# Gating units summed in PSUM from the first, the output norm moved ahead of them, and the next layer's shift read inside the last turn of branch a

## The chip, the cores and the metric

One core of one Trainium2 chip runs the whole program. The metric is the device time of that core in microseconds (us). The engines are TensorE (PE), VectorE (DVE), ScalarE (ACT), GpSimd (POOL) and SyncE (SP), which here only issues DMAs.

## What is computed

Two layers of a trunk with three branches, on 256 tokens of width 2048. Cut to what matters for the change:

```python
cond = jax.nn.silu(c)
for layer in range(DEPTH):                       # 2
    shift, scale, gate = split(cond @ w_ada[layer] + b_ada[layer])   # each 2048 wide
    h = rms_norm(x, norm_g[layer]) * (1.0 + scale) + shift
    ... = split_columns(h @ w_in[layer])         # a: delta rule, b: convolution, c: attention
    y_a = rms_norm(o_a, gdn_norm_g[layer]) * silu(z_a)
    y_b = silu(layer_norm(u, ...)) * silu(z_b)
    y_c = o_c * silu(z_c)
    merged = g_a * (y_a @ w_proj_a) + g_b * (y_b @ w_proj_b) + g_c * (y_c @ w_proj_c)
    x = x + gate * (merged @ w_out[layer])
```

The change touches three things: `cond @ w_ada` for `gate` (called GATING in the kernel) of each layer, where its first four row blocks are summed; the place of the output norm of `y_a`; and the place where the next layer's `shift` is read.

## The kernel before

**The weight stream.** All big products go over weights of 512 KB a slot (256 rows by 512 columns), in a ring of four buffers: SP loads `raw` (L365, once `w_split` says that the slot's last user on POOL is done), ACT rounds it to `wh` (L524, once PE has used the slot four back), POOL subtracts to get `wl` (L503, counts `w_split`), and PE multiplies three times (L864 to L866, counts `w_used`). A group over the model width is eight slots, a projection is four. All engines walk the 672 slots in the same written order. SP's queue is in order: whatever it waits for, all later loads wait behind it.

**The z groups and the branches.** In each layer, behind branch c, come two groups for z_b, two for z_a (`z_silu(4)` and `z_silu(5)` on DVE are for these), then four turns of branch b and four of branch a. A turn is a gate group of eight slots and a projection of four. DVE adds the gate bias when the gate group is done (`gate_add`, L1624), ACT takes its tanh (`gate_tanh`), which frees the PSUM banks of pair 0, and DVE merges (`merge`, L1637 and L1639). ACT rounds four slots ahead of PE, so `gate_tanh` of a turn stands behind its rounding of that turn's four projection slots.

**The conditioning units.** `cond @ w_ada` is summed on DVE, one block of 128 rows at a time: `mod_unit` (L1352 to L1362) waits for a 1 MB block in `modw0` or `modw1`, multiplies it by a column of `cond` and adds it to a running sum of 128x2048. The sum lies in PSUM (`ps[:, 4:8]`, called wide) or in SBUF (`acc`, called side). Units 0 to 3 go from SBUF to SBUF, on a sum set to zero first; unit 4 (`UNIT_A`) reads SBUF and writes PSUM; 5 to 14 stay in PSUM; 15 goes back to SBUF. Each counts `mod_used`. SP issues the load of block n (`mod_load`, L373 to L378) once unit n-2 has counted, because there are two buffers, and these loads stand in the same queue as the weight stream:

- blocks 0 and 1 of GATING in the last z_a group; blocks 2 and 3 behind slot 1 of the first gate group of b, blocks 4 and 5 behind its slot 5, 6 and 7 behind slot 1 of the projection, and so on;
- in the last turn of a of layer 0, the units of the next layer's SCALE: blocks 0 and 1 behind slots 1 and 5 of the gate group, 2 and 3 behind slot 1 of the projection.

Between them lies DVE's written order. Ahead of the b turns it is: `o_recip(0)` (half of the reciprocal for the output norm, L1801), a memset, `z_silu(4)`, the last steps of y_b (L1808, L1810), units 0 and 1, `o_recip(1)`, the output norm's multiply (L1816), `yl` (L1819), `z_silu(5)`, the multiply of y_a (L1822), units 2 and 3. In the last a turn of layer 0 it is: a wait for `mod_summed` and the read of the shift (L1366), a memset, units 0 and 1, `gate_add`, three `merged_low` (L1869), units 2 and 3, `merge`.

`mod_summed` comes from PE, which adds the 128 partitions of `acc` up with 16 small products (`mod_sum`, L958) ahead of the last slot (`MOD_T = 14`) of the gate group of that last turn. In the projection of that turn PE also turns the merged rows (`turn_merged`, L1269): the first before its second half slot, once `gate_tanh` has freed pair 0; the second needs `shift_taken` too, since the shift lies in the bank that it writes.

Of the kernel before, what the change touches and what calls it, by code (L numbers as in the profile page):

```python
# [20 lines left out]
ALU = mybir.AluOpType  # L21
# [107 lines left out]
def trunk(nc, xt, cvec, rel_bias, w_ada, w_in, w_pa, w_pb, w_pc, w_out, b_gate, params, consts, hot, out):  # L129
    ctx = ExitStack()  # L130
    with ctx:
# [1170 lines left out]
        def _(dve):  # L1302
# [49 lines left out]

            def mod_unit(kt, u, s, which, last=KT - 1):

                V.drain()
                dve.wait_ge(mod_landed[s], (u - s) * 8 + 16)
                side = acc[:, which].rearrange("p (b n) -> p b n", b=4)
                wide = ps[:, 4:8, :]
                V.scalar_tensor_tensor(wide if UNIT_A <= kt < last else side,  # L1359
                                       modw[s][:].rearrange("p (b n) -> p b n", b=4), cond[:, kt:kt + 1],  # L1360
                                       wide if UNIT_A < kt <= last else side, ALU.mult, ALU.add
                                       ).then_inc(sem("mod_used"), 1)  # L1362

# [30 lines left out]
            for layer in range(DEPTH):  # L1394
# [405 lines left out]
                def o_recip(half):  # L1800
                    V.reciprocal(ors[:, 4 * half:4 * half + 4], ors[:, 4 * half:4 * half + 4])  # L1801

                dve.wait_ge(sem("o_rms"), L1)
                o_recip(0)
                V.memset(acc[:, 0], 0.0)
                z_silu(4, 0, zs[0])
# [3 lines left out]
                V.scalar_tensor_tensor(ub[:], ub[:], 0.25, zs[1][:], ALU.mult, ALU.mult).then_inc(sem("yb_ready"), 1)  # L1810
                for n in (0, 1):
                    mod_unit(n, passes[0] + n, n % 2, 0)

                o_recip(1)
                V.drain()
                V.scalar_tensor_tensor(qg, qg, p_(layer, "gdn_g"), ors[:], ALU.mult, ALU.mult)  # L1816
                done("o_normed")
                dve.wait_ge(sem("yh_ready"), 3 * layer + 2)
                V.tensor_tensor(yl[:], ub[:], yh[:].bitcast(F32), ALU.subtract).then_inc(sem("y_split"), 1)  # L1819
                z_silu(5, 1, zs[0])  # L1820
                hc += 4 * G_IN
                V.scalar_tensor_tensor(qg, qg, 0.5, zs[0][:], ALU.mult, ALU.mult).then_inc(sem("ya_ready"), 1)  # L1822
                for n in (2, 3):
                    mod_unit(n, passes[0] + n, n % 2, 0)

                def turn(i, br, n0, last_a=False):

                    plan = turn_units(layer, br, i == 3)
                    if plan:
                        l, part, kt = plan  # L1830
                        at = passes[(part + 1) % 3] + kt
                        k0 = 0 if i == 3 else i * 4
                        if i == 3:
                            V.memset(acc[:, 1 - part], 0.0)
                    def units(first):
                        for n in range(first, first + 2):
                            if plan:
                                mod_unit(k0 + (kt + n), k0 + (at + n), n % 2, 0 if part == GATING else 1 - part)

                    units(0)  # L1840
                    gate_add(i, hc, n0)
                    if last_a:
                        return units
                    units(2)
# [14 lines left out]
                for i in range(3):  # L1859
                    turn(i, "a", 12 * layer + 8)  # L1860
                    merge(i, hc, 12 * layer + 8, False)
                if not last_layer:
                    dve.wait_ge(sem("mod_summed"), 3 * layer + 2)
                    mods_from(layer + 1, SHIFT).then_inc(sem("shift_taken"), 1)
                units = turn(3, "a", 12 * layer + 8, True)
# [71 lines left out]
```

## Time and profile before

| | |
|---|---|
| median of three runs | 2473.62 us (2473.61 to 2476.98) |
| the profiled execution | 2470.99 us, of which the span is 2469.2 us |
| granted TensorE clock, mean | 0.959 of full speed |
| instructions | 37923 |
| bytes moved | 479.83 MB, mean 194 GB/s |

The page of the profile gives busy time by engine; the timeline gives the instructions of one engine in order, merged where alike, with the idle time ahead in brackets and what ended it; the chain of waits groups idle time by who was waited for. SPq is SP's own queue: its rows are DMA issues. A row of the stretches view gives busy us of each engine with the number of instructions, then the granted clock, the share of the DMA engines' time and the rate.

### The profile page before, as it was taken

What the parts mean: (1) busy time and instruction counts of PE and PEld (TensorE: products, weight loads), DVE (VectorE), ACT (ScalarE), POOL (GpSimd) and SP (SyncE); (2) the same over time, 40 slices, a digit from 0 to 9 for tenths busy, and PEclk for the clock granted to TensorE, in tenths of its full rate; (3) what the DMA queues carried; (4) which work ended last, traced back from release to release, by engine and by line L of the source; (5) the groups of instructions that cost most, each with busy time, mean ns of one, the idle gap of its engine ahead of it and who ended that gap; (6) DMA issues with size and microseconds to landing.
All of it is one profiled execution on the core that took longest, in us unless ns stands there. A gap on an engine that the chain in (4) does not pass through costs nothing.

```text
span 2469.2 us, 37923 instructions
## 1 busy us (share of the span) xinstructions
PE 2293.0 (93%) x15224; PEld 2098.9 (85%) x15224; DVE 1250.3 (51%) x1742; ACT 949.4 (38%) x1014; POOL 1674.1 (68%) x676
## 2 busy tenths in 40 slices
PE   3789899989999979998896999998999999899999
PEld 3679899978889968786896999998788998688899
DVE  6749874745443474543434694764545437421110
ACT  2234344472332534343333444436423234344442
POOL 1358768755554778986775886876555558798876
PEclk7789999999999999999998999999999999999999
DMA  8877535443333569797774574554334335975664
GB/s 329 319 252 224 162 121 178 146 132 121 124 119 103 179 244 323 279 319 263 289 249 148 186 218 143 167 168 130 124 123 128 111 114 194 323 272 187 200 209 154
DMA packets 228326, 479.83 MB, mean 194 GB/s; under 512 B 21569, under 2 KB 25793, under 8 KB 219617
## 3 DMA queue, kind: packets, MB, share of 16 engines
q1 hardware_dynamic: 226880, 475.72, 57.2%
q8 instruction: 96, 1.57, 0.3%
q10 hardware_dynamic: 1312, 2.23, 0.2%
q14 instruction: 38, 0.30, 0.0%
HBM read 471.48 MB, written 6.29 MB: 193 GB/s over the span
## 4 chain that ended last, share of the span: by engine, by line
POOL 47%; issue 40%; PE 12%; POOLq 1%; DMA 0%; ACT 0%; DVE 0%; DVEq 0%; ACTq 0%
POOL wl L503 47%; PE ps L864 4%; PE ps L865 4%; PE ps L866 4%; POOLq L502 0%; PE ps L958 0%; DMA raw<-w_pb 0%; PE ps L1269 0%; POOLq L498 0%; ACT wh L524 0%; ACT gate L512 0%; DVE xs L1889 0%; DVE ps L1624 0%; POOLq L503 0%; DVEq L1307 0%
## 5 line engine op out<-in xcount | busy, mean ns | idle before, releaser
L503 POOL TENSOR_TENSOR wl<-raw,wh 128x1024 fp32r<-128x1024 f32 x672 | 1673.9, 2504 | 782.1 <-ACT wh L524 780.7
L524 ACT CAST wh<-raw 128x1024 fp32r<-128x1024 f32 x672 | 701.0, 1048 | 1275.2 <-PE ps L866 994.9
L864 PE MATMUL ps<-ah,wh 128*128 128x256 f32 x3008 | 873.3, 290 | 49.9 <-DVE al L1404 36.2
L865 PE MATMUL ps<-al,wh 128*128 128x256 f32 x3008 | 859.9, 286 | 0.0
L866 PE MATMUL ps<-ah,wl 128*128 128x256 f32 x3008 | 859.5, 286 | 0.0
L864 PEld LDWEIGHTS ps<-ah,wh 128*128 128x128 f32 x3008 | 587.0, 195 | 57.5 <-issue 22.5
L865 PEld LDWEIGHTS ps<-al,wh 128*128 128x128 f32 x3008 | 586.8, 195 | 4.7 <-issue 4.4
L866 PEld LDWEIGHTS ps<-ah,wl 128*128 128x128 f32 x3008 | 586.3, 195 | 0.0
L864 PE MATMUL ps<-wh,ah 128*128 128x512 f32 (+1 forms) x832 | 327.0, 393 | 28.1 <-POOL wl L503 28.1
L866 PE MATMUL ps<-wh,al 128*128 128x512 f32 (+1 forms) x832 | 320.0, 385 | 0.0
L865 PE MATMUL ps<-wl,ah 128*128 128x512 f32 (+1 forms) x832 | 319.9, 385 | 0.0
L864 PEld LDWEIGHTS ps<-wh,ah 128*128 128x128 f32 x832 | 158.3, 190 | 60.7 <-POOL wl L503 32.8
L1453 DVE SCALAR_TENSOR_TENSOR ps<-upad,par,ps 128x256 f32<-128x256 f32 x480 | 199.6, 484 | 9.0
L866 PEld LDWEIGHTS ps<-wh,al 128*128 128x128 f32 x832 | 158.0, 190 | 31.6
L865 PEld LDWEIGHTS ps<-wl,ah 128*128 128x128 f32 x832 | 158.3, 190 | 28.1
L864 PE MATMUL ps<-wh,yh 128*128 128x512 f32 x384 | 157.6, 411 | 2.1 <-POOL wl L503 2.1
L865 PE MATMUL ps<-wl,yh 128*128 128x512 f32 x384 | 151.6, 395 | 0.0
L866 PE MATMUL ps<-wh,yl 128*128 128x512 f32 x384 | 151.3, 394 | 0.0
L1624 DVE TENSOR_TENSOR ps<-ps,gbias 128x1024 f32<-128x1024 f32 x24 | 29.5, 1230 | 195.4 <-PE ps L866 195.4
L1359 DVE SCALAR_TENSOR_TENSOR ps<-modw,cond,ps 128x2048 f32<-128x2048 f32 x37 | 87.1, 2355 | 34.4 <-DMA modw<-w_ada 29.9
L1347 DVE SCALAR_TENSOR_TENSOR ps<-adaw,cond,ps 128x512 f32<-128x512 f32 x112 | 84.6, 755 | 9.2 <-issue 0.5
L864 PEld LDWEIGHTS ps<-wh,yh 128*128 128x128 f32 x384 | 73.5, 191 | 17.9 <-POOL wl L503 4.4
(254 smaller groups left out, 2057.7 us busy)
## 6 DMA issues: line engine op xcount, KB each, us to landing
raw<-w_in SPq DMA_DIRECT2D x512, 512.0 KB, 3.4
modw<-w_ada SPq DMA_DIRECT2D x64, 1024.0 KB, 5.7
adaw<-w_ada SPq DMA_DIRECT2D x32, 1024.0 KB, 7.5
raw<-w_out SPq DMA_DIRECT2D x64, 512.0 KB, 4.7
raw<-w_pc SPq DMA_DIRECT2D x32, 512.0 KB, 3.6
raw<-w_pb SPq DMA_DIRECT2D x32, 512.0 KB, 8.1
raw<-w_pa SPq DMA_DIRECT2D x32, 512.0 KB, 4.9
gbias<-b_gate SPq DMA_DIRECT2D x24, 256.0 KB, 4.2
```

What stands on the lines that cost most here:

```text
L503: nc.gpsimd.tensor_tensor(wl[:, s], raw[:, s], wh[:, s].bitcast(F32), ALU.subtract).then_inc(sem("w_split"), 1)
L524: A.copy(wh[:, s], raw[:, s]).then_inc(sem("w_rounded"), 1)
L864: M.matmul(o, lh, rh, start=start, stop=False, skip_group_check=True)
L865: M.matmul(o, lh, rr, start=False, stop=False, skip_group_check=True)
L866: return M.matmul(o, ll, rh, start=False, stop=last, skip_group_check=True)
L1347: u = V.scalar_tensor_tensor(o, adaw[j][:, m], cond[:, kt:kt + 1], wide, ALU.mult, ALU.add)
L1359: V.scalar_tensor_tensor(wide if UNIT_A <= kt < last else side, modw[s][:].rearrange("p (b n) -> p b n", b=4), cond[:, kt:kt + 1], wide if ...
L1453: V.scalar_tensor_tensor(o, upad[:, ct, back:back + T], w, o, ALU.mult, ALU.add)
L1624: V.tensor_tensor(ps[:, 0:2, :], ps[:, 0:2, :], spread(gbias[:], 1, [P, TT, GW]), ALU.add).then_inc(sem("gate_sum"), 1)
```

## The change

`mod_unit` gets an argument `first`, the unit from which the sum lies in PSUM: 0 for GATING, still `UNIT_A` for SHIFT and SCALE. Unit 0 of every pass becomes a plain multiply, and the memsets that set the sums to zero go, ahead of the b turns and in the last turn of b and a. The output norm goes ahead of `z_silu(4)`, units 0 and 1 stay where they were, unit 2 goes ahead of `z_silu(5)`, unit 3 stays. The read of the next layer's shift goes behind the first two units of the last a turn.

```diff
-            def mod_unit(kt, u, s, which, last=KT - 1):
+            def mod_unit(kt, u, s, which, last=KT - 1, first=UNIT_A):
                 V.drain()
                 dve.wait_ge(mod_landed[s], (u - s) * 8 + 16)
                 side = acc[:, which].rearrange("p (b n) -> p b n", b=4)
                 wide = ps[:, 4:8, :]
-                V.scalar_tensor_tensor(wide if UNIT_A <= kt < last else side,
-                                       modw[s][:].rearrange("p (b n) -> p b n", b=4), cond[:, kt:kt + 1],
-                                       wide if UNIT_A < kt <= last else side, ALU.mult, ALU.add
-                                       ).then_inc(sem("mod_used"), 1)
+                o = wide if first <= kt < last else side
+                w = modw[s][:].rearrange("p (b n) -> p b n", b=4)
+                if kt == 0:
+                    unit = V.tensor_scalar(o, w, cond[:, 0:1], None, ALU.mult)
+                else:
+                    unit = V.scalar_tensor_tensor(o, w, cond[:, kt:kt + 1], wide if first < kt <= last else side,
+                                                  ALU.mult, ALU.add)
+                unit.then_inc(sem("mod_used"), 1)
...
+                def gating_units(*n):
+                    for m in n:
+                        mod_unit(m, passes[0] + m, m % 2, 0, first=0)
+
                 dve.wait_ge(sem("o_rms"), L1)
                 o_recip(0)
-                V.memset(acc[:, 0], 0.0)
+                o_recip(1)
+                V.drain()
+                V.scalar_tensor_tensor(qg, qg, p_(layer, "gdn_g"), ors[:], ALU.mult, ALU.mult)
                 z_silu(4, 0, zs[0])
...
-                for n in (0, 1):
-                    mod_unit(n, passes[0] + n, n % 2, 0)
-
-                o_recip(1)
-                V.drain()
-                V.scalar_tensor_tensor(qg, qg, p_(layer, "gdn_g"), ors[:], ALU.mult, ALU.mult)
-                done("o_normed")
+                gating_units(0, 1)
                 dve.wait_ge(sem("yh_ready"), 3 * layer + 2)
                 V.tensor_tensor(yl[:], ub[:], yh[:].bitcast(F32), ALU.subtract).then_inc(sem("y_split"), 1)
+                gating_units(2)
                 z_silu(5, 1, zs[0])
                 hc += 4 * G_IN
                 V.scalar_tensor_tensor(qg, qg, 0.5, zs[0][:], ALU.mult, ALU.mult).then_inc(sem("ya_ready"), 1)
-                for n in (2, 3):
-                    mod_unit(n, passes[0] + n, n % 2, 0)
+                gating_units(3)
...
-                        if i == 3:
-                            V.memset(acc[:, 1 - part], 0.0)
...
-                                mod_unit(k0 + (kt + n), k0 + (at + n), n % 2, 0 if part == GATING else 1 - part)
+                                mod_unit(k0 + (kt + n), k0 + (at + n), n % 2, 0 if part == GATING else 1 - part,
+                                         first=0 if part == GATING else UNIT_A)
 
                     units(0)
+                    if last_a and layer < DEPTH - 1:
+                        dve.wait_ge(sem("mod_summed"), 3 * layer + 2)
+                        mods_from(layer + 1, SHIFT).then_inc(sem("shift_taken"), 1)
                     gate_add(i, hc, n0)
...
-                if not last_layer:
-                    dve.wait_ge(sem("mod_summed"), 3 * layer + 2)
-                    mods_from(layer + 1, SHIFT).then_inc(sem("shift_taken"), 1)
                 units = turn(3, "a", 12 * layer + 8, True)
```

## Rows read from the trace of the kernel before

**Rows 1.** The page's first part: busy us, share of the span, instructions.
```profile
PE 2293.0 (93%) x15224; PEld 2098.9 (85%) x15224; DVE 1250.3 (51%) x1742; ACT 949.4 (38%) x1014; POOL 1674.1 (68%) x676
```

**Rows 2.** SP's own waits, whole span: us, times, longest.
```profile
SPq L377 <- DVE acc L1359: 85.3, 15, 16.7
```

**Rows 3.** PE's waits, the stretch 825 to 945 us, then 2030 to 2150 us.
```profile
PE ps L864 <- POOL wl L503: 14.6, 6, 8.9
...
PE ps L864 <- POOL wl L503: 14.6, 6, 8.8
```

**Rows 4.** SPq's timeline ahead of layer 0's first b turn: start, us, issues.
```profile
867.59 4.75 SPq L377 DMA_DIRECT2D modw<-w_ada  x2
872.39 7.01 SPq L365 DMA_DIRECT2D raw<-w_in  x4
894.33 4.71 SPq L377 DMA_DIRECT2D modw<-w_ada  x2
899.09 0.95 SPq L365 DMA_DIRECT2D raw<-w_in  x2
```

**Rows 5.** DVE's timeline in the same stretch.
```profile
834.85 6.55 DVE L1801 RECIPROCAL ors<-ors 128x1024 f32<-128x1024 f32 x1 [3.63 <-ACT ors L797]
...
855.05 1.22 DVE L1608 SCALAR_TENSOR_TENSOR zs<-zt,ps 128x1024 f32<-128x1024 f32 x1 [11.51 <-ACT zt L512]
...
863.25 8.72 DVE L1359 SCALAR_TENSOR_TENSOR acc<-modw,cond,acc 128x2048 f32<-128x2048 f32 x2
...
881.27 4.28 DVE L1819 TENSOR_TENSOR yl<-ub,yh 128x2048 fp32r<-128x2048 f32 x1
...
886.83 3.10 DVE L1822 SCALAR_TENSOR_TENSOR qkv<-qkv,zs 128x2048 f32<-128x2048 f32 x1
890.04 8.63 DVE L1359 SCALAR_TENSOR_TENSOR acc<-modw,cond,acc 128x2048 f32<-128x2048 f32 x2
```

**Rows 6.** The unit's forms on DVE: ns least/median/most, first and last start.
```profile
L1359 DVE SCALAR_TENSOR_TENSOR ps<-modw,cond,ps x37: 2354/2355/2358, 903.5 to 2188.6; 128x2048 f32<-128x2048 f32 x37
L1359 DVE SCALAR_TENSOR_TENSOR acc<-modw,cond,acc x19: 2350/4259/4320, 863.3 to 2099.5; 128x2048 f32<-128x2048 f32 x19
```

**Rows 7.** POOL's subtraction: all of them, then four in the stretch of rows 5.
```profile
L503 POOL TENSOR_TENSOR wl<-raw,wh x672: 2332/2403/4477, 38.5 to 2454.0; 128x1024 fp32r<-128x1024 f32 x168
...
879.39 17.14 POOL L503 TENSOR_TENSOR wl<-raw,wh 128x1024 fp32r<-128x1024 f32 x4 [0.38 <-ACT wh L524]
```

**Rows 8.** ACT's timeline in the same stretch.
```profile
880.56 1.01 ACT L512 ACTIVATE zt<-ps 128x1024 f32<-128x1024 f32 x1
...
904.95 1.04 ACT L524 CAST wh<-raw 128x1024 fp32r<-128x1024 f32 x1 [20.21 <-DMA raw<-w_in]
```

**Rows 9.** Stretches of 5 us: busy (x) of PE, PEld, DVE, ACT, POOL; clock, DMA.
```profile
890.00:895.00 5.00, 3.64 (x16) 2.55 (x14) 4.85 (x2) 0.00 (x0) 5.00 (x2) 1.00 0.02 3
...
905.00:910.00 5.00, 1.54 (x4) 1.25 (x5) 0.84 (x1) 2.12 (x3) 3.93 (x2) 0.50 1.00 302
```

**Rows 10.** PE's wait in layer 0's last a turn, 1130 to 1210 us.
```profile
PE ps L1269 <- ACTq L735: 12.3, 1, 12.3
```

**Rows 11.** SPq's timeline there.
```profile
1142.27 2.73 SPq L365 DMA_DIRECT2D raw<-w_pa  x2
1161.74 2.78 SPq L377 DMA_DIRECT2D modw<-w_ada  x2
```

**Rows 12.** DVE's timeline there.
```profile
1135.85 1.22 DVE L1639 TENSOR_TENSOR mtok<-mtok,ps 128x1024 f32<-128x1024 f32 x1
1156.97 0.17 DVE L1366 TENSOR_TENSOR mods<-ps,par 128x16 f32<-128x16 f32 x1 [19.90 <-PE ps L958]
...
1159.36 4.79 DVE L1359 SCALAR_TENSOR_TENSOR acc<-modw,cond,acc 128x2048 f32<-128x2048 f32 x2
1164.08 1.23 DVE L1624 TENSOR_TENSOR ps<-ps,gbias 128x1024 f32<-128x1024 f32 x1
```

**Rows 13.** A stretch behind the wait of rows 10, columns as in rows 9.
```profile
1174.00:1178.00 4.00, 2.95 (x11) 2.76 (x12) 0.00 (x0) 0.95 (x2) 3.42 (x2) 0.50 0.96 399
```

## The prediction

> **What bounds the kernel now.** I read the page first. PE is busy 93% of the span and POOL, which has to subtract every weight slot before PE may use it, 68% [rows 1]. So no engine is full, and what the change can win is PE's idle time. Then I read SP's own waits: its load of the conditioning blocks stood 85.3 us behind units that DVE sums in SBUF, 16.7 us at the longest [rows 2]. While it stands there, no weight is loaded. Then PE's waits in three stretches: around the first b turn of layer 0 and of layer 1 PE's products waited 14.6 us for POOL, each time, 8.9 us of it at once [rows 3], and in the last a turn of layer 0 PE's turning waited 12.3 us for ACT's queue [rows 10]. The timelines say what lay behind both.
>
> *Ahead of the b turns.* SP may load blocks 2 and 3 only when units 0 and 1 have counted. These run from 863.25 to 871.97 on DVE [rows 5], so SP issues them at 867.6 and 872.0, and the next weights at 872.39 [rows 4]. Then come blocks 4 and 5, which need units 2 and 3: these run from 890.04 to 898.67, behind `o_recip(1)`, the norm, `yl`, `z_silu(5)` and the y_a multiply [rows 5]. SP issues weights until 879.40, and the next at 899.09 [rows 4]: 19.7 us without a weight load. ACT sits 20.21 us for it, until 904.95 [rows 8]. Between 890 and 895 us the DMA engines are at 0.02 of their time [rows 9]. So this is a wait and no shortage of bandwidth.
>
> *In the last a turn.* DVE is free at 1137.1, but its next instruction is the shift, for which it waits 19.90 us until PE has summed it, at 1156.97 [rows 12]. Units 0 and 1 stand behind, at 1159.36, and SP's load of block 2 behind unit 0. SP's weights stop at 1145.0 and go on behind 1164.5 [rows 11]. So projection slots 2 and 3 come late, ACT's tanh stands behind rounding them, and PE's first turn behind the tanh.
>
> **The change part by part.**
>
> *Units 0 and 1 of GATING in PSUM.* A unit from SBUF to SBUF takes 4.259 us in the median, one from PSUM to PSUM 2.355, always [rows 6]. The least of the SBUF form, 2.350, shows that the instruction itself is no longer; the rest is DVE and POOL in each other's way, for POOL's subtraction takes 2.403 in the median and 4.28 (17.14 / 4) in this stretch [rows 7]. The new unit 0 is a form that no row has, a plain multiply from SBUF to PSUM. Between zero and 4.32 (the most of rows 6) I take 2.36, for it moves the same 2048 elements with one input fewer. Units 0 and 1 then end at 863.25 + 2 x 2.36 + 0.1 = 868.1 instead of 872.0: SP goes on 3.9 us earlier, and the weights behind it too.
>
> The Trainium skill (SBUF — State Buffer, Who interferes with whom) says that a VectorE instruction with two SBUF inputs and a GpSimd one that reads SBUF lock each other out for the whole instruction. By that a contended pair would cost 2.36 + 2.40 = 4.76 us, where the rows show 4.26 and 4.28. The sum with it would be some 1 us better a layer for the units and 1.6 us worse for the y_a multiply, so it changes little; the measurement is used.
>
> *Output norm ahead of `z_silu(4)`.* Added there are 6.55 us for `o_recip(1)` [rows 5] and the multiply; L1822, of the same size, took 3.10. Together 9.65, under the 11.51 us for which DVE sat idle ahead of `z_silu(4)` [rows 5], with a memset less besides. So nothing in front. If that cover were gone, y_b and all behind it would be late by the excess, at most the 9.65. Behind units 0 and 1 it takes these 9.2 to 9.65 us out of DVE's order.
>
> *Unit 2 ahead of `z_silu(5)`.* DVE: `yl` from 868.2 to 872.5 (4.28, it is contended), then unit 2 to 874.9 if block 2 has landed. It is issued at 865.9 instead of 867.6. So unit 2 has counted before SP comes to block 4, which stands behind weight slots whose buffers come free only at about 877.5 (879.4 less some 2). Price: nothing, as `z_silu(5)` waits for its tanh meanwhile.
>
> *What is late next.* `z_silu(5)` needs ACT's tanh, which began at 880.56 [rows 8] behind the rounding of weights that SP had issued late. These come 3.9 us earlier at best. I take the tanh 3 us earlier, so over at 878.6, with the bounds 877.7 and 881.6 (not earlier at all). Then `z_silu(5)` 1.22, the y_a multiply 3.10, unit 3 2.36 and 0.3 between them: unit 3 counts at 885.6 (884.7 to 888.6) instead of 898.67. SP, which stood before block 5, and all the weights behind it go on **13.1 us earlier**, bounds 10.1 and 14.0. PE must also have used up what it had by then: it lost 1.9 us a slot to the four contended subtractions [rows 7], of which only one, under the y_a multiply, is left, so PE is some 5 to 7 us ahead there and still has to wait a little. From here each load, unit and slot follows the other as before, in DMA queues that fill as before [rows 9]. I take 12.5 a layer, a little under the 13.1, for a multiply that is contended in full. Layer 1 has the same instructions and waits [rows 3], so 2 x 12.5 = **25.0 us**, bounds 20 and 28.
>
> After 9 us of idle PE's clock was at 0.50 of full speed, the lower of its two levels, between 905 and 910 us [rows 9]. With an idle time of some 3 us it may stay up, and one weight slot less run at half speed. That would be about 1.8 us a layer. I leave it out of the sum, since the projection slots behind then wait for loads in a full queue, and keep it for the range: 3.6.
>
> *The shift inside the turn.* Units 0 and 1 of SCALE now start at 1137.1, as their blocks stand in SP's queue ahead of the weights of 1142.27 [rows 11] and units 14 and 15 of SHIFT have long been done. They are still summed in SBUF, at 4.32 each at most, so they count by 1141.4 and 1145.8, and SP is at that point from 1145.0 [rows 11]: its stop of 16.7 us becomes 1 us or none. Then DVE waits for the sum, reads the shift at 1156.97 as before, and is free for `gate_add`, which in the trace began at 1164.08 behind two units [rows 12]. PE had gate slot 7 left behind the sum: 12 products, some of them at half clock, to about 1160.3. Then `gate_add` 1.23, the tanh 1.02 and 0.3 of semaphores: pair 0 is free at 1162.8, and PE comes there at 1162.4. The wait of 12.3 [rows 10] goes, all but 0.4: 11.9. Behind it PE ran at half clock to about 1178, 2.95 us busy in the stretch to there [rows 13]; at full clock half of 3.4 us is saved, 1.7. Together **13.6 us**, once, as layer 1 has no next shift. Bounds: 11.9 without the clock, 14.0; 8 if projection slot 3 lands late behind blocks 2 and 3. The turned rows, the merges and units 2 and 3 behind follow as before.
>
> *What costs nothing.* The memsets and the plain multiply of unit 0 of SHIFT and SCALE lie where DVE waits for PE anyway. New contention of SCALE's units with POOL in the middle of the gate group is at most 2 x 1.9 = 3.8 us of POOL time, and PE has four slots in hand there and stops for the shift's sum just behind. If that cover were gone, up to 3.8 us of the 13.6 would be given back.
>
> The sum: 25.0 + 13.6 = 38.6 us. The profiled execution, 2470.99 (span 2469.2 and 1.8 around it), becomes 2432.4. The median shown is 2.63 above it, 2473.62, and becomes **2435.0**.
>
> **The rivals.**
> (A) *The tanh sets it.* `z_silu(5)` comes no earlier and unit 3 keeps SP: 10 us a layer and 11.9, 32 together: 2442. For it: two orders in a row stand before that tanh (rounding, then PE's use of the slots).
> (B) *One of the two gains fails.* The transfers behind a stop are near the DMA limit (1.00 of the time at 905 to 910 [rows 9]), so a stop that is taken away might come back as slower loads, or the last a turn might be held by `turn_merged` through another wait. Against: at 890 to 895 us the DMA engines were idle [rows 9], so there is room. Time: 2474 less 14 to 25, 2449 to 2460.
> (C) *More than the sum.* The clock stays up in both layers, and each tanh comes at its earliest: 2 x (14.0 + 1.8) + 14.0 = 45.6: 2428.
> (D) *Slower.* Unit 2 now stands ahead of `z_silu(5)` and waits for block 2. Were that block late, `z_silu(5)`, the y_a multiply, unit 3, block 5 and every weight behind would be late with it. It takes over from the gain if block 2 lands more than 12.5 + 13.6 / 2 = 19.3 us behind 872.5, at 891.8, and gives slower by 0.2% at 894.3, 28 us behind its issue. Speaks against it: block 2 landed in the trace before DVE needed it, and nothing but one block and a few slots is in flight. At 896, 2481.
> (E) *It does not do what it says.* SP might wait for something else at the same places, such as POOL's slots: 2474. Against: rows 2 name the SBUF units.
>
> **How the numbers follow.** The sum as told 0.52, A 0.17, B 0.11, C 0.16, D 0.02, E 0.02. The range from 2426 to 2449 takes in the first, A, C and the edge of B, some 8 in 10 with room for what I mis-size. This measurement can tell about 0.2% (5 us) from no change. Faster by more: all but D and E, 0.96; the same 0.02; slower 0.02.
>
> **What the profile of the changed kernel would show.** The SBUF form of the unit falls from 19 to about 9 and its PSUM forms rise. SP's block loads no longer stand 16.7 us behind anything. ACT's wait of 20.2 us falls to some 8. PE's wait for POOL falls from 14.6 to about 4 in both stretches, and its wait for ACT's queue in the last a turn goes. `z_silu(5)` ends about 3 us earlier against the start of the stretch. The prediction is wrong if `z_silu(5)` waits for DVE and not for the tanh, if block 5 is not the load on which SP stands last, or if the time per b turn grows over that of before.

## The result, and the profile after

| | before | changed |
|---|---|---|
| median | 2473.61 us (2473.53 to 2476.98, 4 runs) | 2441.73 us (2438.42 to 2445.06, 4 runs) |
| profiled execution | 2470.99 us, span 2469.2 | 2438.42 us, span 2436.6 |
| ratio of the times | | 0.9872, 95% interval 0.9859 to 0.9884 |

The change makes the kernel 31.9 us faster, where 38.6 were forecast. The profiled execution is the fastest of the four; the spans differ by 32.6 us. The same kernel timed twice more gave 2439.19 (2438.16 to 2447.13) and 2440.78 (2439.86 to 2443.51), and the kernel before, timed beside it, 2473.96 (2469.75 to 2478.14, 11 runs) and 2474.57 (2467.65 to 2476.90, 9 runs). So the gain was 34.8 and 33.8 us the other two times. Differences of 3 us between single kernels are within what either does by itself. Each of the three timings left one profile; the one shown here is the first, and where the other two differ from it the text says so.

The page's first part of the changed kernel, against [rows 1]: PE has the same work, DVE 26 us less.

```profile
PE 2289.7 (94%) x15224; PEld 2098.6 (86%) x15224; DVE 1224.0 (50%) x1738; ACT 949.9 (39%) x1014; POOL 1665.8 (68%) x676
```

The unit's forms on DVE (ns least/median/most), against [rows 6]. There are ten SBUF forms fewer. The first of GATING, a plain multiply into PSUM, takes 2.355 us, as estimated from its neighbour. The first of SHIFT and SCALE, which stays in SBUF, takes 1.8.

```profile
L1364 DVE SCALAR_TENSOR_TENSOR ps<-modw,cond,ps x45: 2354/2356/2357, 868.3 to 2155.0; 128x2048 f32<-128x2048 f32 x45
L1364 DVE SCALAR_TENSOR_TENSOR acc<-modw,cond,acc x9: 2350/2624/4327, 995.8 to 1258.3; 128x2048 f32<-128x2048 f32 x9
...
L1362 DVE TENSOR_SCALAR ps<-modw,cond x2: 2355/2355/2355, 865.8 to 2049.8; 128x2048 f32<-128x2048 f32 x2
L1362 DVE TENSOR_SCALAR acc<-modw,cond x2: 1793/1807/1821, 989.5 to 1130.3; 128x2048 f32<-128x2048 f32 x2
```

SP's own waits over the whole span, against [rows 2] and, as the first line, the row of before for the units in PSUM. Behind units summed in SBUF 17.2 us are left of 85.3, behind units in PSUM it is 78.9 for 63.5, so 96.1 for 148.8 together. The last wait has moved with the unit, and the longest is half as long.

```profile
SPq L377 <- DVE ps L1359: 63.5, 21, 5.5
...
SPq L377 <- DVE ps L1364: 78.9, 25, 8.4
...
SPq L377 <- DVE acc L1364: 17.2, 5, 5.3
```

PE's waits from 825 to 945 us (layer 0) and from 2010 to 2130 us (layer 1), against [rows 3]. Both layers began with 14.6 us. Layer 0 keeps half of it, layer 1 little over a quarter. In the other two profiles of the changed kernel it is 6.0 and 6.3 us, and 6.4 and 5.4, so the difference between the layers is of this execution.

```profile
PE ps L864 <- POOL wl L503: 7.4, 2, 6.1
...
PE ps L864 <- POOL wl L503: 4.1, 4, 1.5
```

**Ahead of layer 0's first b turn.** SP's queue, against [rows 4]. The trace runs 0.8 us late by the silu ahead of it (855.81 for 855.05), so weights go on behind block 5 at 890.00 for 899.09, 9.9 us earlier; forecast was 13.1.

```profile
868.41 2.58 SPq L377 DMA_DIRECT2D modw<-w_ada  x2
871.11 9.54 SPq L365 DMA_DIRECT2D raw<-w_in  x4
880.69 9.26 SPq L377 DMA_DIRECT2D modw<-w_ada  x2
890.00 0.94 SPq L365 DMA_DIRECT2D raw<-w_in  x2
```

DVE's timeline there, against [rows 5], with POOL's and ACT's rows under it.

```profile
848.65 3.48 DVE L1815 SCALAR_TENSOR_TENSOR qkv<-qkv,par,ors 128x2048 f32<-128x2048 f32 x1
855.81 1.22 DVE L1612 SCALAR_TENSOR_TENSOR zs<-zt,ps 128x1024 f32<-128x1024 f32 x1 [3.68 <-ACT zt L512]
857.18 4.11 DVE L1818 SCALAR_TENSOR_TENSOR ub<-lnt,ub 128x2048 f32<-128x2048 f32 x1
...
865.80 2.35 DVE L1362 TENSOR_SCALAR ps<-modw,cond 128x2048 f32<-128x2048 f32 x1
...
875.30 2.36 DVE L1364 SCALAR_TENSOR_TENSOR ps<-modw,cond,ps 128x2048 f32<-128x2048 f32 x1 [2.06 <-DMA modw<-w_ada]
882.34 1.22 DVE L1612 SCALAR_TENSOR_TENSOR zs<-zt,ps 128x1024 f32<-128x1024 f32 x1 [4.69 <-ACT zt L512]
883.71 3.43 DVE L1827 SCALAR_TENSOR_TENSOR qkv<-qkv,zs 128x2048 f32<-128x2048 f32 x1
887.23 4.81 DVE L1364 SCALAR_TENSOR_TENSOR ps<-modw,cond,ps 128x2048 f32<-128x2048 f32 x2
```

```profile
849.94 4.46 POOL L503 TENSOR_TENSOR wl<-raw,wh 128x1024 fp32r<-128x1024 f32 x1
```

```profile
879.08 1.05 ACT L524 CAST wh<-raw 128x1024 fp32r<-128x1024 f32 x1 [5.22 <-DMA raw<-w_in]
...
881.29 1.02 ACT L512 ACTIVATE zt<-ps 128x1024 f32<-128x1024 f32 x1
...
897.77 1.04 ACT L524 CAST wh<-raw 128x1024 fp32r<-128x1024 f32 x1 [10.49 <-DMA raw<-w_in]
```

Three things are to be seen. The norm's multiply fits its gap, as said: DVE still waits 3.68 us ahead of the first silu. But it meets POOL, takes 3.48 us, and the subtraction beside it takes 4.46, where 2.403 is the median [rows 7]. POOL comes out of that some 2 us late; it works back to back, and is in the middle of a subtraction when the y_b step L1818 begins. That step takes 4.11 us. POOL's rows there:

```profile
854.36 4.78 POOL L503 TENSOR_TENSOR wl<-raw,wh 128x1024 fp32r<-128x1024 f32 x2
...
859.11 4.45 POOL L503 TENSOR_TENSOR wl<-raw,wh 128x1024 fp32r<-128x1024 f32 x1
```

In the kernel before POOL had a pause ahead of its next subtraction, the step came in first, and the subtraction stretched instead; DVE's row and POOL's:

```profile
856.41 2.33 DVE L1808 SCALAR_TENSOR_TENSOR ub<-lnt,ub 128x2048 f32<-128x2048 f32 x1
```

```profile
857.05 3.94 POOL L503 TENSOR_TENSOR wl<-raw,wh 128x1024 fp32r<-128x1024 f32 x1 [0.47 <-ACT wh L524]
```

So the one that begins first runs at its own pace, and the other stands until it is through: the step from 857.18 waits for the subtraction that ends at 854.36 + 4.78 = 859.14 and ends 2.15 us behind it, at 861.29. This is what the Trainium skill says (SBUF — State Buffer, Who interferes with whom): the lock is held for a whole instruction, and the order of issue decides who blocks.

So units 0 and 1 begin 1.8 us later than the old order would have it, and SP, whose weights wait for POOL, reaches block 2 late. Second, the tanh begins at 881.29 for 880.56 [rows 8]: with the 0.8 us taken off, not earlier at all. The silu behind it begins 3.9 us earlier even so (882.34 for 885.48): in the kernel before it waited for its turn on DVE, and only now for the tanh. Third, the y_a multiply took 3.43, and unit 3 ends at 889.6.

Layer 1 has the same instructions, but in this execution the y_a multiply wins there against POOL. POOL's subtraction ahead of it ends at 2066.64, just as the multiply begins, and the multiply takes 2.31 us. In layer 0 the subtraction runs to 884.98, the multiply begins at 883.71 in the middle of it, and takes 3.43. Tanh and multiply together let unit 3 end 2.3 us earlier in layer 1, against the first silu (31.5 us behind 2039.82, and 33.8 behind 855.81). This was luck: in the other two profiles the multiply of layer 1 took 4.37 and 3.94 us. POOL's rows of layer 0 and 1, then DVE's of layer 1, the last line from the second profile:

```profile
882.57 2.41 POOL L503 TENSOR_TENSOR wl<-raw,wh 128x1024 fp32r<-128x1024 f32 x1
...
2064.23 2.41 POOL L503 TENSOR_TENSOR wl<-raw,wh 128x1024 fp32r<-128x1024 f32 x1
```

```profile
2066.48 2.31 DVE L1827 SCALAR_TENSOR_TENSOR qkv<-qkv,zs 128x2048 f32<-128x2048 f32 x1
2068.90 4.81 DVE L1364 SCALAR_TENSOR_TENSOR ps<-modw,cond,ps 128x2048 f32<-128x2048 f32 x2
...
2065.27 4.37 DVE L1827 SCALAR_TENSOR_TENSOR qkv<-qkv,zs 128x2048 f32<-128x2048 f32 x1
```

SP's row of layer 1, and the clock of both layers in stretches of 3 us where the weights are short (columns as in rows 9), layer 0 first, then layer 1, then layer 1 of the second profile:

```profile
2064.72 6.91 SPq L377 DMA_DIRECT2D modw<-w_ada  x2
```

```profile
896.00:899.00 3.00, 0.00 (x0) 0.00 (x0) 2.36 (x1) 1.05 (x2) 0.11 (x1) 0.77 0.81 261
...
2080.00:2083.00 3.00, 1.94 (x8) 1.61 (x9) 0.00 (x0) 0.89 (x1) 3.00 (x2) 1.00 1.04 363
...
2083.00:2086.00 3.00, 3.00 (x8) 2.31 (x7) 0.00 (x0) 1.72 (x2) 2.19 (x2) 0.50 1.04 433
```

In layer 0 PE stops for 6.1 us and its clock falls to the lower level, 1.2 GHz; in layer 1 it stops for 1.5 at most and stays at 2.4. In the other two profiles PE stops for 4.7 and 4.3 us, and for 5.2 and 4.2, and the clock falls in both layers each time. `gate_add` of the first b turn comes at 908.58 for 916.22 and at 2086.90 for 2121.17; counted from the silu ahead, layer 0 gains 8.4 us and layer 1 14.0 up to there. In the other two profiles it is 9.5 and 8.9, and 7.9 and 9.0. What is gained there need not last: of the 5.0 us by which layer 1 of this profile is ahead of the second one at `gate_add`, 1.2 are left at the end of the span.

**The last a turn of layer 0.** SP's queue, against [rows 11]; DVE, against [rows 12]; and PE's wait, against [rows 10].

```profile
1136.76 4.86 SPq L365 DMA_DIRECT2D raw<-w_pa  x2
1141.67 0.94 SPq L377 DMA_DIRECT2D modw<-w_ada  x2
```

```profile
1130.30 1.82 DVE L1362 TENSOR_SCALAR acc<-modw,cond 128x2048 f32<-128x2048 f32 x1 [0.28 <-issue]
...
1150.65 0.17 DVE L1370 TENSOR_TENSOR mods<-ps,par 128x16 f32<-128x16 f32 x1 [11.68 <-PE ps L958]
1155.05 1.23 DVE L1628 TENSOR_TENSOR ps<-ps,gbias 128x1024 f32<-128x1024 f32 x1 [4.22 <-PE ps L866]
```

```profile
PE ps L1269 <- ACTq L735: 1.1, 1, 1.1
```

SP's stop of 16.7 us is gone (the two block loads take 0.94 us), and PE's wait falls from 12.3 to 1.1. `gate_add` stands 4.40 us behind the shift's read; the prediction had 3.3 for the slot between (1156.97 to about 1160.3). In the trace of before that slot's products end at 1160.8 and not at 1160.3, so 0.5 us of it was misread.

### The profile page after: what moved, and what is told of

Same layout as the page of the kernel before. It is cut to its first block, busy times and chain, and to the rows that moved or that the text cites. A ratio compares the mean times of both kernels' runs of the same rounds, so it can differ in the third digit from the quotient of the medians.

```text
span 2436.6 us, 37917 instructions
## 1 busy us (share of the span) xinstructions
PE 2289.7 (94%) x15224; PEld 2098.6 (86%) x15224; DVE 1224.0 (50%) x1738; ACT 949.9 (39%) x1014; POOL 1665.8 (68%) x676
## 4 chain that ended last, share of the span: by engine, by line
POOL 46%; issue 39%; PE 14%; POOLq 1%; DVE 0%; ACT 0%; DVEq 0%; ACTq 0%
POOL wl L503 46%; PE ps L864 5%; PE ps L865 5%; PE ps L866 5%; POOLq L502 0%; PE ps L958 0%; PE ps L1269 0%; POOLq L498 0%; DVE xs L1892 0%; DVE ps L1628 0%; ACT wh L524 0%; ACT gate L512 0%; POOLq L503 0%; DVEq L1307 0%; ACTq L735 0%
## 5 line engine op out<-in xcount | busy, mean ns | idle before, releaser
L864 PE MATMUL ps<-ah,wh 128*128 128x256 f32 x3008 | 873.7, 290 | 50.5 <-DVE al L1408 36.7
L864 PEld LDWEIGHTS ps<-wh,ah 128*128 128x128 f32 x832 | 157.8, 190 | 38.7 <-POOL wl L503 10.9
L1364 DVE SCALAR_TENSOR_TENSOR ps<-modw,cond,ps 128x2048 f32<-128x2048 f32 x45 | 106.0, 2356 | 39.0 <-DMA modw<-w_ada 33.8
```

The costliest lines, as they stand in the source:

```text
L864: M.matmul(o, lh, rh, start=start, stop=False, skip_group_check=True)
L1364: unit = V.scalar_tensor_tensor(o, w, cond[:, kt:kt + 1], wide if first < kt <= last else side, ALU.mult, ALU.add)
```

## The experiments

Each was timed against the kernel before on the same chip.

**The change again**, timed beside the next three.

> The changed kernel once more, as the reference for the three others on this chip. If its spread of 6.6 us in four runs (2438.42 to 2445.06) comes from whether TensorE's clock falls in the first b turn, as it does in the profiled run in layer 0 (0.77 in the stretch 896 to 899 us) and not in layer 1, the profile here shows one, both or none of the two falls, and the time goes with it, some 2 to 4 us for each. If the spread is of the chip and not of the kernel, the kernel before shows it too.

Measured: 2439.19 us (2438.16 to 2447.13), ratio 0.987 (0.9854 to 0.9885). One of its five runs lies 5 us above the next, while the kernel before spreads over 8.4 us beside it. The profile shows both falls (0.50 at 901 to 903 us and at 2083 to 2086), and the profiled execution took 2438.16 us, where the first one, with one fall, took 2438.42. So the guess of 2 to 4 us for each fall is not borne out, and the kernel before has the spread too.

**The shift alone.** Kernel before, with

```diff
                     units(0)
+                    if last_a and layer < DEPTH - 1:
+                        dve.wait_ge(sem("mod_summed"), 3 * layer + 2)
+                        mods_from(layer + 1, SHIFT).then_inc(sem("shift_taken"), 1)
                     gate_add(i, hc, n0)
...
-                if not last_layer:
-                    dve.wait_ge(sem("mod_summed"), 3 * layer + 2)
-                    mods_from(layer + 1, SHIFT).then_inc(sem("shift_taken"), 1)
```

> The kernel before with the shift's read inside the last a turn and nothing else. My theory: the stop of SP's queue in that turn is a matter of its own, worth 11 to 14 us (13.6 in the prediction, 11.5 read from the distance of the two traces), so 2460 to 2463. Rival: part of it shows only because the b turns before it were moved, then it is under 9.

Measured: 2463.94 us (2459.26 to 2468.97), ratio 0.996 (0.9945 to 0.9975): 10.0 us. DVE's rows of its profile show where the missing 3.6 went: the shift is read at 1158.78, 1.8 us later than in [rows 12], and `gate_add` comes 5.4 us behind it, not 3.3.

```profile
1158.78 0.17 DVE L1366 TENSOR_TENSOR mods<-ps,par 128x16 f32<-128x16 f32 x1 [12.01 <-PE ps L958]
1164.18 1.23 DVE L1624 TENSOR_TENSOR ps<-ps,gbias 128x1024 f32<-128x1024 f32 x1 [5.22 <-PE ps L866]
```

ACT's row and two stretches of the same profile (columns as in rows 9) show two places. Raw weights for gate slot 6 come 2.70 us after ACT wants them, and PE has a gap (2.65 busy of 4). Blocks 2 and 3 are not the cause, for SP issues them at 1149.43, behind that. POOL's twelve subtractions of this turn took 32.45 us, where they took 28.37 before; this is the meeting of SCALE's units with POOL for which the prediction would give back up to 3.8. Whether it, or the DMA, made the shift late was not tried by itself. The changed kernel's three profiles have the read only 0.1 to 0.7 us later than before, counted from the last `merge`, where this one has 2.1. The other place is behind the shift's sum. There the clock is at 0.50 for the whole of gate slot 7, and its twelve products take 5.3 us; before, they took 4.0, with the clock at 0.50 for about half of them.

```profile
1145.68 1.05 ACT L524 CAST wh<-raw 128x1024 fp32r<-128x1024 f32 x1 [2.70 <-DMA raw<-w_in]
```

```profile
1146.00:1150.00 4.00, 2.65 (x12) 1.90 (x11) 0.77 (x1) 2.52 (x3) 4.00 (x2) 1.00 0.42 134
...
1158.00:1162.00 4.00, 4.00 (x12) 3.32 (x13) 0.17 (x1) 0.73 (x1) 0.34 (x1) 0.50 1.10 442
```

**GATING alone.** The changed kernel with the shift's read back in its old place (the edit above, turned round).

> The changed kernel with the shift's read put back. My theory: what is left is the gating part, 8 us in layer 0 and 12 in layer 1 by the two traces, 20 to 21 together, so 2452 to 2455. The prediction had 25.0. The sum of this run's gain and that of the run with the shift alone should be that of the change, within 2 us, if the two parts are independent.

Measured: 2452.39 us (2448.57 to 2459.56), ratio 0.9919 (0.9904 to 0.9934): 21.6 us. With the 10.0 of the shift that is 31.6; the whole change gave 34.8 beside them and 31.9 the first time. The sum misses the 34.8 by 3.2 us, more than the 2 expected, but the interval of that 34.8 is 28 to 36, so within the spread the two parts add. Put the other way, on top of the other part the shift gave 13.2 us and GATING 24.8.

Not all of the 21.6 is GATING's. The edit also takes the memset from the units of SHIFT and SCALE and makes their unit 0 a plain multiply. In the last a turn of layer 0 these stand behind the shift's read here, and SP's block 2 behind them. The turn takes 59.5 us from the last `merge` before it to its first `merge` in this run and in the next one, where it took 62.1 before: 2.6 us, for a part that the prediction put at nothing. With the read inside the turn too it is 49.8, 49.7 and 49.2 in the three profiles of the changed kernel, and 52.2 in the run with the shift alone. DVE's row from the next run, with POOL idle:

```profile
1150.34 1.28 DVE L1362 TENSOR_SCALAR acc<-modw,cond 128x2048 f32<-128x2048 f32 x1
```

**The sums in PSUM, in the old order.** The kernel before with the new `mod_unit`. All memsets go, so this is one thing more than the expectation says:

```diff
                 o_recip(0)
-                V.memset(acc[:, 0], 0.0)
                 z_silu(4, 0, zs[0])
...
-                for n in (0, 1):
-                    mod_unit(n, passes[0] + n, n % 2, 0)
+                gating_units(0, 1)
...
-                for n in (2, 3):
-                    mod_unit(n, passes[0] + n, n % 2, 0)
+                gating_units(2, 3)
```

> The kernel before with one thing changed: GATING's units 0 to 3 are summed in PSUM, unit 0 as a plain multiply without the memset; the order on VectorE is the old one. By the unit's rows it takes 3.9 us off units 0 and 1 and again off units 2 and 3, so SP stands 3.9 us less at block 3 and some 6 us less at block 5: my theory is a gain of 5 to 8 us a layer, 10 to 16 together, 2458 to 2463. Rival: the order is what gives the gain, and PSUM alone gives under 5 together, because the loads behind block 3 come no earlier while the DMA queue is full.

Measured: 2452.24 us (2450.80 to 2457.07), ratio 0.9915 (0.99 to 0.9929): 21.7 us, above the 10 to 16 expected even without the 2.6 of the last a turn, and as much as the whole gating part. The rival, that the order gives the gain, falls. SP's and DVE's rows of it:

```profile
887.92 2.80 SPq L377 DMA_DIRECT2D modw<-w_ada  x2
890.77 0.94 SPq L365 DMA_DIRECT2D raw<-w_in  x2
```

```profile
857.39 2.33 DVE L1815 SCALAR_TENSOR_TENSOR ub<-lnt,ub 128x2048 f32<-128x2048 f32 x1
...
878.76 2.28 DVE L1823 TENSOR_TENSOR yl<-ub,yh 128x2048 fp32r<-128x2048 f32 x1
```

In layer 0 the stop before block 5 ends at 890.77, where the new order has 890.00; in layer 1 it ends 36.9 us behind the first silu, where the new order has 34.2 in three of four profiles with it (31.8 in the first). Units 2 and 3 both stand behind the y_a multiply here, and still layer 0 is as early. With units 0 and 1 out of POOL's way, POOL had finished the slots that it had; it began its next at 878.86, so `yl` came in first, and took 2.28 us for 4.28 [rows 5]. In layer 1 it took 4.49. Units 2 and 3 save 3.8 us more. And the y_b step takes 2.33, for the 4.11 of the changed kernel. What freeing POOL gives was undersized in my sum, and what the order gives was oversized.

**Norm back, unit 2 back, old order with the shift inside.** The changed kernel with one move undone, the other, and both.

```diff
# norm back
+                gating_units(0, 1)
                 o_recip(1)
                 V.drain()
                 V.scalar_tensor_tensor(qg, qg, p_(layer, "gdn_g"), ors[:], ALU.mult, ALU.mult)
# unit 2 back
-                gating_units(2)
                 z_silu(5, 1, zs[0])
...
-                gating_units(3)
+                gating_units(2, 3)
```

> The changed kernel with the second half of the reciprocal and the output norm's multiply back behind units 0 and 1. In the changed kernel the multiply ahead of the z_b silu met POOL, took 3.48 us, made POOL late (six subtractions in 20.39 us), and the y_b step behind took 4.11 instead of 2.33, so units 0 and 1 began 1.8 us later than they could. My theory: put back, units 0 and 1 begin 1.8 us earlier, but yl and unit 2 come 9.2 us later; unit 2 then ends near 884, z_silu(5) waits for it some 2 to 4 us, and with it unit 3 and block 5: 2 to 4 us a layer slower than the changed kernel, 4 to 8 together. Rival: the contention costs as much as the place gives, then no difference within 2 us or a gain.

> The changed kernel with unit 2 back behind the y_a multiply, next to unit 3. VectorE waits 4.7 us for the tanh in either case, so unit 2 costs 2.4 us behind the multiply instead of nothing: unit 3 and block 5 2.4 us later, and block 4 issued some 8 us later. My theory: 2 to 4 us a layer slower than the changed kernel, 4 to 8 together. Rival: block 4 late makes unit 4 late and SP stands a second time at block 6: 10 or more together.

> The changed kernel with VectorE's old order ahead of the b turns: output norm behind units 0 and 1, units 2 and 3 both behind the y_a multiply; the sums in PSUM from unit 0 and the shift inside the turn stay. With the shift put back, the order made no difference at all (2452.39 with the new order, 2452.24 with the old one). My theory now: the new order's gain (unit 2 for nothing) is eaten by the norm multiply's contention with POOL, so this kernel is the changed one within 3 us, 2438 to 2445. Rival: with the shift in place the order does matter, since the runs with the norm back (2445.84) and unit 2 back (2444.22) were 4 to 6 us slower than the changed kernel; then this is 2446 to 2450.

Measured: norm back 2445.84 us (2444.20 to 2454.78; ratio 0.9896, 0.9879 to 0.9914), unit 2 back 2444.22 (2441.78 to 2452.18; 0.9886, 0.9869 to 0.9902), both back 2445.55 (2443.16 to 2448.95; 0.9882, 0.9866 to 0.9898), with the changed kernel beside the last one at 2440.78 (0.9867, 0.9851 to 0.9884). The medians say that the two moves are worth some 3 to 6 us, and only together, as one undone costs as much as both. The intervals of the ratios overlap, and without the shift the order was worth nothing (2452.39 and 2452.24). So the order's worth is between 0 and 5 us, and these runs don't settle it closer. The profiles say what each move does to the stop before block 5, which ends 34.2 us behind the first silu in the changed kernel (31.8 once, as said). With unit 2 back it ends at 36.7 and 36.6 in the two layers, the 2.4 us later that were expected; with the norm back at 34.6 and 36.9, and with both back at 34.7 and 37.0. So unit 2's place matters next to nothing once the norm is back.

**The changed kernel again**, beside the last two.

> The changed kernel again, as the reference on this chip for the two others: 2439 to 2442.

Measured: 2440.78 us (2439.86 to 2443.51).

**Unit 3 ahead of the silu too.**

```diff
-                gating_units(2)
+                gating_units(2, 3)
                 z_silu(5, 1, zs[0])
...
-                gating_units(3)
```

> The changed kernel with unit 3 ahead of z_silu(5) as well. In the trace VectorE sits idle there from 877.7 to 882.3 us, and unit 3 takes 2.36, so it hides, and SP's block 5 no longer waits for the tanh and the y_a multiply. It stood from 881.0 to 889.6 in layer 0 and 65.1 to 71.3 (2000 more) in layer 1. If the tanh is what sets the stop, as the prediction's first rival has it, this is worth 6 to 9 us a layer, 12 to 17 together: 2425 to 2430. If the DMA queue is what sets it (it runs at 0.8 to 1.0 of its time from 869 to 884), the loads come no earlier and it is under 6 together.

Measured: 2431.66 us (2431.62 to 2435.83), ratio 0.9833 (0.9819 to 0.9846): 42.2 us, some 7 to 10 more than the changed kernel, between the two bounds. It was timed beside other kernels than the changed one, but the intervals of the two ratios don't meet. SP's and ACT's rows:

```profile
881.08 0.94 SPq L377 DMA_DIRECT2D modw<-w_ada  x2
883.04 2.75 SPq L365 DMA_DIRECT2D raw<-w_in  x2
```

```profile
890.72 1.05 ACT L524 CAST wh<-raw 128x1024 fp32r<-128x1024 f32 x1 [5.13 <-DMA raw<-w_in]
```

SP no longer stops at block 5, and its weights go on at 883.04, 7.0 us earlier than 890.00. ACT's wait falls from 10.49 to 5.13, and the rest of it is the DMA's. So in the changed kernel the tanh and the y_a multiply did set that stop. Not all that is won there is kept: `gate_add` comes 7.9 us earlier than in the first profile (44.9 us behind the silu for 52.8), but from there to `merge` it is 14.1 us for 10.9.

**The norm's multiply late**, the reciprocal left early.

```diff
                 o_recip(1)
-                V.drain()
-                V.scalar_tensor_tensor(qg, qg, p_(layer, "gdn_g"), ors[:], ALU.mult, ALU.mult)
                 z_silu(4, 0, zs[0])
...
                 gating_units(2)
+                V.scalar_tensor_tensor(qg, qg, p_(layer, "gdn_g"), ors[:], ALU.mult, ALU.mult)
                 z_silu(5, 1, zs[0])
```

> The changed kernel with only the output norm's multiply moved, from ahead of the z_b silu to between unit 2 and z_silu(5), into the 4.7 us in which VectorE waits for the tanh; both reciprocals stay early. If the multiply's contention with POOL is what made units 0 and 1 1.8 us late, they now begin 1.8 us earlier, POOL keeps up, and the change gains 1.5 to 2 us a layer, 3 to 4 together. If the tanh or the DMA queue sets the stop anyway, nothing changes within 1.5 us.

Measured: 2434.69 us (2432.32 to 2438.43), ratio 0.9844 (0.983 to 0.9857), 4.5 to 7 us better than the changed kernel by the medians, where 3 to 4 were expected; the two were not timed together, and the intervals of their ratios touch, so the size is not sure. Its y_b step is short again, and weights behind block 5 go on at 888.27 for 890.00, 2.1 us earlier against the first silu. The tanh now comes 1.7 and 2.4 us earlier than before in the two layers:

```profile
857.52 2.31 DVE L1816 SCALAR_TENSOR_TENSOR ub<-lnt,ub 128x2048 f32<-128x2048 f32 x1
```

So the multiply cost the time that it kept from POOL, though it stood in a gap of DVE's.

**Both.**

> The changed kernel with unit 3 ahead of z_silu(5) and the output norm's multiply between unit 3 and z_silu(5). Alone, the first gave 2431.66 and the second 2434.69, against 2439.19 to 2441.73 of the changed kernel. If they are independent (one frees SP from the y_a multiply, the other begins the units 1.8 us earlier) they add: 2425 to 2429. If unit 3 and the multiply compete for the few us in which VectorE waits for the tanh (unit 2, unit 3 and the multiply are 7.1 us from 874, so until 881.4, with the tanh over at 881.0), z_silu(5) is just late and nothing is lost, for block 5 is already free. Rival: with block 5 free the DMA queue or the weights' own supply sets the time, then no better than 2431.

Measured: 2433.61 us (2429.52 to 2435.64), ratio 0.9835 (0.982 to 0.985). It is no better than unit 3 ahead alone; the rival holds. The weights there go on 27.6 us behind the first silu, against 26.8, so with block 5 free there is nothing for the earlier units to win. The fastest kernel of this case is that with unit 3 ahead, 1.7% under the kernel before; it and this one can't be told apart.

## Why the prediction was right in kind, and its gain 4 to 7 us too large

**The mechanism** was right: in both places SP's queue stood behind a unit on DVE and held the weight stream. By and large the kernels whose stop before block 5 ends earlier are the faster ones, though not by as much. With the shift's read inside the turn, the old order ends the stop 34.7 and 37.0 us behind the silu in the two layers and takes 2445.55 us, and unit 3 ahead ends it at 26.8 in both and takes 2431.66: 18 us of stop are worth 14. The change gained 31.9, 34.8 and 33.8 us in its three timings, where 38.6 were forecast. The first of them, 2441.73, is the 2442 of rival A.

**The term that was mis-sized** is that of GATING, 25.0 us (12.5 a layer). It measured 21.6 alone with the 2.6 of the last a turn in it, so 19.0. The profiles say the same. The first two columns of gains are GATING's (from the first silu of layer 0 to the last `merge` before the last a turn, and from the first silu of layer 1 to the end), the middle one holds the last a turn and what follows up to layer 1's silu. Each line is one execution, in us; the kernel before has 280.8, 924.3 and 409.1.

| gain over before | layer 0 | last a turn and on | layer 1 |
|---|---|---|---|
| changed, first | 7.8 | 13.2 | 12.3 |
| changed, second | 9.7 | 12.6 | 11.1 |
| changed, third | 9.6 | 12.9 | 8.9 |
| shift alone | -0.5 | 6.0 | 0.5 |
| GATING alone | 10.7 | 1.6 | 10.7 |
| sums in PSUM, old order | 8.3 | 3.9 | 7.6 |

In the changed kernel GATING's two layers give 18.5 to 20.8 us, not 25.0. Three steps of its working failed, the first in part because of the second.

- "I take the tanh 3 us earlier." In the three profiles of the changed kernel it came between 0.2 later and 1.3 earlier, which was rival A (10.1 us a layer): weights behind block 5 go on 9.6 to 9.9 us earlier, and 12.2 once. The rounding ahead of the tanh waits for raw weights (the 5.22 us ahead of 879.08), and these landed when they had before: with 0.8 taken off 879.08 it is 878.3, for 878.26. They were issued only 2.1 us earlier by the same count, where 3.9 were forecast, because the norm's multiply had made POOL and units 0 and 1 late by 1.8. With that multiply moved they were issued 3.8 us earlier and landed 1.6 earlier. What else holds them back is probably the DMA queue, which is at 1.00 of its time from 869 to 878 us, with blocks 2 and 3 within 2.6 us of each other ahead of them; that was not tried by itself.
- "So nothing in front", of the output norm. I checked it against DVE's idle time only. Its cover on DVE was there, but it lengthened one subtraction of POOL by 2.1 us, and that made the next DVE step 1.8 us longer. The run with the multiply moved into another gap puts the price at 4.5 to 7 us for both layers, by medians that were not taken side by side.
- "From here each load, unit and slot follows the other as before". They did not: what is ahead at `gate_add` is partly lost behind it, as the second profile and the run with unit 3 ahead show.

**Unit 0 to 3 in PSUM** were right in their price (2.36), and they are nearly the whole of GATING's gain: 21.7 us in the old order, the 2.6 included. I had given the units 3.9 us and counted the moves for the rest. The runs showed the other way round: 0 to 5 us for the moves, and more for a free POOL.

**The clock** was left out of the sum and put into the range. In the first profile it stayed up in layer 1 and fell in layer 0, where PE stopped 6.1 us and not the 3 I had expected; in the other two it fell in both layers, and the whole time was not longer for it in one of them (2438.16) and 3 us longer in the other (2441.63). What a fall costs was not tried by itself.

**The shift**, 13.6 us forecast, measured 10.0 alone and 13.2 on top of the other part. With the wait of 12.3 down to 0.9 in the run with the shift alone, 11.4 are won, and 1.7 behind it, where the clock is now at full speed: from the end of the wait to the first `merged_low` it is 4.6 us for 6.3. Given back were 3.2, as PE comes there later: 2.1 in the gate group, and the rest in gate slot 7, which ran at half clock throughout, where I had taken only "some of them at half clock". That leaves the 9.9 which the turn shows. Part of the 12.3 us that the same turn gains in the changed kernel can be the memset and the plain multiply, which I had put at nothing; the runs don't part the two there.

**The rivals.** B, D and E fell: the stops that were taken away did not come back as large, block 2 was waited for by only 2.06 us, and SP's waits were what they were said to be. C fell too, as the clock fell in layer 0. A came true in what it said of the tanh, and its 2442 is the time that was measured first; that its 10 and 11.9 us add up so well is luck too, for the other two timings are 1 to 3 us below it.

The range of 2426 to 2449 held the time. The sentence that weighed the lock of the Trainium skill (SBUF — State Buffer, Who interferes with whom) against the rows was right to change little, but wrong to set it against the measured 4.26. The lock holds: the y_b step ends 2.15 us behind the subtraction, where it takes 2.33 alone, so some 0.2 us of it ran beside the other. Twice that off the 4.76 is 4.4, an estimate, and two contended units took 8.72 [rows 5]. What I missed in it is that who blocks is decided by who comes first, so the same multiply takes 2.31 or 3.43, or 4.37 in the second profile.

## What to carry to other kernels

An in-order DMA queue that mixes two streams stops the greater for the lesser. Look for the unit on which its last load waits, and ask what stands ahead of that unit on its engine: here one unit moved ahead of a wait for another engine was worth 7 to 10 us, more than all moves of the change. Filling an idle gap of VectorE with an instruction of two SBUF inputs is not free while GpSimd works, whatever VectorE's own slack; charge it to GpSimd and to the VectorE step behind. And read more than one profile before explaining why two layers differ: here the other two profiles of the same kernel did not show it.

## What the runs showed of the hardware

- A two-input VectorE instruction of 128x2048 in SBUF and POOL's subtraction of 128x1024 run one after the other where both are at it: up to 4.1 to 4.5 us for the one that comes second, 2.35 and 2.40 alone. Which of the two is stretched is decided by some tenths of a us.
- With the sum in PSUM the same instruction takes 2.354 to 2.357 us in all 45 cases, whatever POOL does.
- A plain multiply of 128x2048 by a column, SBUF to SBUF, took 1.28 us with POOL idle (old place of the shift's read) and 1.79 to 1.82 with POOL at work; from SBUF to PSUM 2.355.
- One such meeting makes the next: the norm's multiply ended 5.0 us before the y_b step began (852.13 and 857.18), and POOL's lateness carried it over.
- PE's clock fell to 1.2 GHz in stops of 4.2 to 6.1 us ahead of `gate_add` of the first b turn, in five of six cases in three profiles of the changed kernel, and stayed at 2.4 GHz in the sixth, with stops of up to 1.5 us.
